# One of two subtractions per slice of the down-projection moves from VectorE to GpSimd

## The reference, cut to what matters

```
def conv_ffn(h, w_up, conv_w, conv_b, w_down):
    u = h @ w_up                       # 1024 x 5632
    c = conv_b + sum over j of conv_w[j] * u shifted by j
    a, g = jnp.split(c, 2, axis=-1)
    return (jax.nn.silu(a) * g) @ w_down      # z (1024 x 2816) @ w_down (2816 x 1024)

x = x + conv_ffn(rmsnorm(x, ffn_norm[l]), w_up[l], conv_w[l], conv_b[l], w_down[l])
```

## Time and profile before

| | |
|---|---|
| time, median of 3 runs | 1670.67 us (1668.64 to 1672.5) |
| the profiled execution: its time, its span | 1670.67 us, 1668.9 us |
| PE busy | 1614.7 us, 97% of the span |
| DVE busy | 1072.7 us, 64% |
| POOL busy | 946.5 us, 57% |
| ACT busy | 708.2 us, 42% |
| down stage: first to last PE matmul of L3146 | about 1454.6 to 1665.7 us |

### The profile page before, as it was taken

The page is one execution under the profiler, slowest core; times in us unless marked ns, Lnnn a source line. Parts: engine busy times, 40 slices in busy tenths (PEclk is TensorE's granted clock), DMA queues, the critical chain, the costliest instruction groups (busy, mean ns, idle before and its releaser), DMA issues.

```text
span 1668.9 us, 22838 instructions
## 1 busy us (share of the span) xinstructions
PE 1614.7 (97%) x8386; PEld 1329.5 (80%) x8386; DVE 1072.7 (64%) x1555; ACT 708.2 (42%) x1268; POOL 946.5 (57%) x705
## 2 busy tenths in 40 slices
PE   6999999998989999999999999999999999999999
PEld 5887878877778787888888887778888888888887
DVE  7555242357876493222655246888888888889897
ACT  5455465544554333333411233434433334454432
POOL 5642656544222287766344556999999999410041
PEclk9999999999999999999999999999999999999999
DMA  6113011002110233332455711222322222497244
GB/s 224 39 60 105 1 39 42 28 12 59 39 37 9 56 109 101 102 107 99 139 159 160 260 64 42 72 89 83 95 76 76 76 89 82 159 343 248 83 141 162
DMA packets 145146, 165.51 MB, mean 99 GB/s; under 512 B 16708, under 2 KB 97292, under 8 KB 145036
## 3 DMA queue, kind: packets, MB, share of 16 engines
q1 hardware_dynamic: 144604, 164.04, 30.5%
q10 hardware_dynamic: 432, 0.01, 0.0%
HBM read 131.40 MB, written 32.62 MB: 98 GB/s over the span
## 4 chain that ended last, share of the span: by engine, by line
PE 57%; POOL 5%; DVE 2%; issue 1%; ACT 0%; POOLq 0%; ACTq 0%
PE ps L3048 23%; PE ps L3146 11%; PE ps L2146 11%; PE ps L2186 7%; PE ps L2202 5%; POOL f_lo L2788 1%; POOL f_lo L1873 1%; PE ps L2137 1%; PE ps L2195 0%; POOL ffn_area L1888 0%; POOL ffn_area L1886 0%; POOL ffn_area L1883 0%; DVE attn_lo L2932 0%; POOL ffn_area L1885 0%; POOL ffn_area L2804 0%
## 5 line engine op out<-in xcount | busy, mean ns | idle before, releaser
L2788 POOL TENSOR_TENSOR f_lo<-ffn_area,f_hi 128x1024 fp32r<-128x1024 f32 x85 | 201.9, 2394 | 20.2 <-ACT f_hi L2663 20.2
L3048 PE MATMUL ps<-t_all,f_hi 128*128 128x512 f32 x528 | 164.3, 392 | 2.8 <-DVE t_all L2815 1.6
L2663 ACT ACTIVATE f_hi<-ffn_area 128x1024 fp32r<-128x1024 f32 x85 | 80.2, 946 | 184.5 <-PE ps L3048 169.8
L3146 PE MATMUL ps<-attn_lo 128*128 128x512 f32 x624 | 143.8, 390 | 0.0
L1873 POOL TENSOR_TENSOR f_lo<-ffn_area,f_hi 128x1024 fp32r<-128x1024 f32 (+1 forms) x42 | 97.5, 2325 | 69.4 <-ACT f_hi L1720 69.4
L3146 PEld LDWEIGHTS ps<-attn_lo 128*128 128x128 f32 x624 | 117.2, 188 | 24.5 <-issue 0.2
L3048 PE MATMUL ps<-act_hi,f_hi 128*128 128x512 f32 x336 | 133.3, 397 | 2.6 <-POOL f_lo L2788 2.6
L690 POOL TENSOR_SCALAR head_rstd<-head_ss 128x8 f32<-128x8 f32 (+2 forms) x42 | 10.4, 247 | 217.0 <-DVE head_ss L981 217.0
L3048 PE MATMUL ps<-act_hi,f_lo 128*128 128x512 f32 x336 | 132.3, 394 | 0.0
L3048 PE MATMUL ps<-act_lo,f_hi 128*128 128x512 f32 x336 | 131.3, 391 | 0.0
L1279 PE MATMUL ps<-w_hi,act_hi 128*128 128x512 f32 (+1 forms) x320 | 122.5, 383 | 5.8 <-DVE w_lo L506 2.6
(11 more groups left out here) (356 smaller groups left out, 4450.8 us busy)
## 6 DMA issues: line engine op xcount, KB each, us to landing
ffn_area<-in_w_up_dram SPq DMA_DIRECT2D x44, 512.0 KB, 5.2
gate<-gates SPq DMA_DIRECT2D x24, 512.0 KB, 3.7
ffn_area<-in_w_gate_dram SPq DMA_DIRECT2D x23, 512.0 KB, 5.1
z<-attn_out SPq DMA_DIRECT2D x22, 512.0 KB, 2.6
gates<-ffn_area SPq DMA_DIRECT2D x40, 256.0 KB, 2.1
t_raw<-in_w_down_dram SPq DMA_DIRECT2D x34, 256.0 KB, 6.3
attn_out<-in_x_dram SPq DMA_DIRECT2D x16, 512.0 KB, 6.2
f_raw<-in_w_down_dram SPq DMA_DIRECT2D x26, 256.0 KB, 4.9
```

Of the source, the lines that this page charges most:

```text
L2663: act.activation(part_place(p, part, f_hi, first_hi), part_source(p, part), ACT.Copy).then_inc(w_hi_done, 1)
L2788: pool.tensor_tensor(part_place(p, part, f_lo, first_lo), part_source(p, part), part_place(p, part, f_hi, first_hi).bitcast(F32), ALU.subt ...
L3048: ins = pe.matmul(out, w, a, start=(start and k == 0 and i == 0), stop=(stop and k == 3 and i == 2))
L3146: ins = pe.matmul(down_bank(i, t), z[a][:, t * P:(t + 1) * P], w[b], start=(k == 0 and n == 0), stop=(k == DEPTH - 1 and n == 2))
```

## The change

`z_low` moves from VectorE's stream to GpSimd's, for all 77 slices. VectorE keeps `w_low`. GpSimd's 20 additions, which stood in one row, now stand between the `z_low` of certain slices: `c11_x1` behind m = 17 to 20, `u3_made` behind m = 50 to 53, `c22_u3` and `c21_x1` in turn behind m = 61 to 68, `c12_x1` behind m = 69 to 72. No instruction is added or taken out, and the streams of TensorE, ScalarE and SyncE are the same instruction by instruction.

```diff
     def gpsimd(pool):
+        def z_low(m):
+            q, k = SLICES[m]
+            pool.wait_ge(z_hi_done, m + 1)
+            pool.tensor_tensor(operand(m, 1), block(DOWN[q], Z_OF[DOWN[q]], k), operand(m, 0).bitcast(F32), ALU.subtract
+                               ).then_inc(z_lo_done, 1)
...
-        for t in range(4):
-            c11_x1(t)
-        for t in range(4):
-            u3_made(t)
-        for t in range(4):
-            c22_u3(t)
-            c21_x1(t)
-        for t in range(4):
-            c12_x1(t)
+        for m in range(len(SLICES)):
+            z_low(m)
+            t = m - at_slice(P2, 0) - RING
+            if 0 <= t < 4:
+                c11_x1(t)
+            t = m - at_slice(P5, 0) - RING
+            if 0 <= t < 4:
+                u3_made(t)
+            n = m - at_slice(P4, 0) - RING
+            if 0 <= n < 8:
+                (c21_x1 if n % 2 else c22_u3)(n // 2)
+            elif 8 <= n < 12:
+                c12_x1(n - 8)
...
     def vector(dve):
-        def z_low(m):
...
-        def both_low(m):
-            z_low(m)
+        for m in range(4):
             w_low(m)
-
-        for m in range(4):
-            both_low(m)
         c12_sum(FT - 1)
         other_taps(FT - 1, 1)
-        both_low(4)
+        w_low(4)
         other_taps(FT - 1, 0)
-        both_low(5)
-        both_low(6)
+        w_low(5)
+        w_low(6)
         product(FT - 1)
         for m in range(7, len(SLICES)):
             combinations(m + AHEAD)
-            both_low(m)
+            w_low(m)
```

## The result

| | before | after |
|---|---|---|
| median of 8 runs | 1669.98 us (1667.15 to 1674.25) | 1679.32 us (1675.04 to 1681.79) |
| profiled execution: its time, its span | 1670.67, 1668.9 us | 1675.62, 1673.8 us |
| down stage, first to last matmul | 211.11 us | 220.70 us |

The ratio of after to before is 1.0052, with a 95% interval of 1.0036 to 1.0067. On 1669.98 us that is +8.7 us (+6.0 to +11.2); the medians themselves lie 9.3 us apart. The forecast was +7.8 us, 1678.5 us, slower with a chance of 0.76.

The account below looks back on a forecast made before the run. TensorE, busy 97% of the span, bounds the kernel; waits of 2.0 + 6.7 = 8.7 us replace 0.9, +7.8 us, so the span goes from 1668.9 to 1676.7, plus 1.8 around it 1678.5 us. Range 1671.5 to 1687.0.

Parts of the forecast that it names:

- The price, 0.60 + 1.11 = 1.71 us a pair: Down stage: VectorE and GpSimd instructions on SBUF take turns, 0.60 us for VectorE's and 1.11 for GpSimd's.
- The rival with a longer turn: Down stage: GpSimd's turn is longer than 1.11 us, so the time is 1684 to 1689 us; chance 0.11.
- Slices 0 to 21: Start of the down stage: TensorE does not wait, and 5 us of lead remain at slice 21.
- lead of `w_low`: Down stage: time from the end of a slice's `w_low` to TensorE's first matmul of it; 11.6 us at slice 60 before.
- Slices 22 to 30, lead 2 and no wait: Two combinations an iteration: 9 x 0.19 us lost, 1.2 for four `c11_y`, lead 2 us left.
- A loss before slice 50: Down stage: TensorE waiting before slice 50 was named as a sign that the forecast is wrong; no size given.
- Slices 31 to 50: Down stage: m = 31 to 41 gain 4.5 us, lead 6.5; m = 42 to 49 lose 1.3 and 0.8, lead 4.4.
- Slices 50 to 55, 2.0 us: At m = 50 to 53, iterations of 4.63 us with `u3_made` use up the lead; TensorE waits 2.0 us.
- Slices 61 to 73, 6.7 us: At m = 61 to 72, a second GpSimd turn loses 0.70 us an iteration; TensorE waits 6.7 us.
- the eight additions of `u4_c22_y` hide mostly under GpSimd's turns: At m = 61 to 72, of these VectorE PSUM additions (4.8 us) only a quarter, 1.2 us, is exposed.
- TensorE waits on `w_low`, not on `z_low`: Near slices 51 to 55 and 62 to 72: waits fall on VectorE's `w_low`, 0.7 us each in the latter.
- Waits saved: Slice 65 of the kernel before: its 0.9 us wait is replaced by the forecast waits of 8.7 us.

Follow-up runs that it names:

- experiment 3: The changed kernel with the four `c11_x1` additions behind m = 23 to 26 in place of 17 to 20; 1676.14 us, ratio 1.0052.
- experiments 4 and 6: GpSimd's 20 additions on VectorE: 4, against the kernel before, `z_low` on VectorE, 1666.53 us; 6, against the changed kernel, `z_low` on GpSimd, 1667.19 us.
- experiment 5: The changed kernel with `w_low` as a multiplication of one SBUF input by 0 in place of the subtraction; 1669.52 us, ratio 0.9999.

## Why the prediction was right, and the step that failed

**The price, 0.60 + 1.11 = 1.71 us a pair: right.** It was taken from four additions beside VectorE. `z_low`, which writes fp32r, steps at the same 1.70 to 1.71 in every stretch shown above. So the 1.30 us of the earlier trace rows was no hint of a longer turn: alone GpSimd steps by 1.25 us, and while both engines compete its part is 1.11. The rival with a longer turn is out.

**Slices 0 to 21: right.** The lead of `w_low` at m = 21 was predicted as 5 and is 4.7 us.

**Slices 22 to 30, lead 2 and no wait: the failed step.** It let GpSimd's 8 instructions up to `z_low(21)` pass, and then took one turn of GpSimd in each iteration, 2.92 us. GpSimd's timeline of the change:

```profile
1490.83 1.30 POOL L2827 TENSOR_TENSOR attn_out<-ffn_area,attn_out 128x512 f32<-128x512 f32 x1 [5.59 <-DMA attn_out<-x_kept]
...
1501.87 1.74 POOL L2821 TENSOR_TENSOR attn_lo<-f_raw,attn_lo 128x512 fp32r<-128x512 f32 x1
1503.57 3.48 POOL L2821 TENSOR_TENSOR t_all<-act_raw,t_all 128x512 fp32r<-128x512 f32 x2
1507.02 5.14 POOL L2821 TENSOR_TENSOR attn_lo<-act_raw,attn_lo 128x512 fp32r<-128x512 f32 x3
```

VectorE's:

```profile
1500.67 1.78 DVE L2936 TENSOR_TENSOR attn_lo<-f_raw,attn_lo 128x512 fp32r<-128x512 f32 x1
...
1505.80 1.80 DVE L2936 TENSOR_TENSOR t_all<-act_raw,t_all 128x512 fp32r<-128x512 f32 x1
...
1510.93 1.77 DVE L2936 TENSOR_TENSOR t_all<-act_raw,t_all 128x512 fp32r<-128x512 f32 x1
```

After `z_low(21)` at 1501.87 come five more without a pause, up to slice 26: GpSimd, held up by 5.59 us for x, still had its four additions to make among the next four `z_low`, and meanwhile ScalarE had written the high parts of the next slices (22 from 1496.44 us on). Until it had caught up, every VectorE instruction had a turn of GpSimd beside it, and an iteration took 3 x 1.71 = 5.13 us (1500.67, 1505.80, 1510.93), a loss of 2.4 each in place of 0.19. The lead of `w_low` fell from 4.7 at m = 21 to 2.3 at 22 and 0.1 at 23, while that of `z_low` grew from 3.5 to 9.3 at m = 26. The engine that isn't late takes turns from the one that is. In the chain above these are the VectorE pieces from 1500.67 on. TensorE lost 1.6 us; experiment 3, which moves the stop, gets it back. A combination that waited 2.0 us for a load stands just ahead (the DMA of the chain, 1485.28 to 1492.10); its part was not tried by itself. A loss before slice 50 was one of the forecast's own signs of being wrong, and here it is one.

**Slices 31 to 50: right.** Lead 5.5 at m = 42 (forecast 6.5 after 41), 4.2 at 49 (4.4).

**Slices 50 to 55, 2.0 us: the mechanism right, the size 3.2.** The iteration with `u3_made` was reckoned as 4.63 us. VectorE's `w_low` shows it:

```profile
1583.62 1.78 DVE L2936 TENSOR_TENSOR attn_lo<-t_raw,attn_lo 128x512 fp32r<-128x512 f32 x1
1585.32 0.68 DVE L2981 TENSOR_TENSOR ffn_area<-ps,ffn_area 128x512 f32<-128x512 f32 x1
...
1588.23 1.78 DVE L2936 TENSOR_TENSOR attn_lo<-t_raw,attn_lo 128x512 fp32r<-128x512 f32 x1
```

4.61 us, and the PSUM addition at 0.68 is indeed exposed. The missing 1.2 us are the steps from slices 53 and 54, 0.69 and 0.62: again `z_low` that had gathered behind an addition (three of them start at 1596.91, 1598.61 and about 1600.3), a second turn in iterations where one was counted.

**Slices 61 to 73, 6.7 us: 6.1.** Lead 3.4 at m = 60 (forecast 2.9), then 0.68 lost in each slice from 65 on, in place of 0.70. That the eight additions of `u4_c22_y` hide mostly under GpSimd's turns held: 3.4 + 6.1 = 9.5 us were used, and 12 x 0.70 + 1.2 = 9.6 were reckoned.

**TensorE waits on `w_low`, not on `z_low`: right** for the matmuls (10 waits). Four weight loads are put down to `z_low`, but each stands 0.03 us ahead of a matmul that waited too, three of them for `w_low`, and the lead of `z_low` was 5.6 us at slice 51 and 2.4 from 66 on: it had long been done.

**Waits saved.** The wait at slice 65 of before, 0.9 us by its row, is 1.2 by the starts. So the stage grew by 10.8 - 1.2 = 9.6 us, 1.8 more than the 7.8 forecast: +1.6 and +1.2 of gathered `z_low`, -0.6 at the end, -0.3 of the wait saved. The measured +8.7 (6.0 to 11.2) holds both. That the median after, 1679.32 us, lies only 0.8 from the forecast is luck in part: the stage lost 1.8 us more than forecast, and the 8 runs of before have a median 0.7 under the 1670.67 that the forecast started from.

## What to carry to other kernels

Where two engines take turns at SBUF, an instruction moved from VectorE costs VectorE the turn of the slower engine: 0.60 us went and 1.11 came. Idle time of the slower engine is no reason to give it more; with fewer instructions on it TensorE lost nothing (experiments 4 and 6). Reckon its turns by what has gathered in front of it, not by one per iteration, since it works off a backlog at the expense of an engine that may be the late one. Measure lost time by the distance of starts; the wait records gave half of it.

## What was unexpected of the hardware

- The one instruction with a single SBUF input that was tried, the `tensor_scalar` of experiment 5, loses the same 1.10 us to GpSimd as those with two: 0.42 becomes 1.52, 0.68 becomes 1.78.
- GpSimd's 128x512 addition of two SBUF inputs steps by 1.25 us alone (1.29 recorded), and adds only 1.11 to VectorE's stream while both are queued: a pair takes 1.71 us, 0.14 less than the 0.60 and 1.25 of the two alone. With a VectorE instruction of 0.33 us (experiment 5) the pair takes 1.44, which is 1.11 again.
- A wait for x or a `u2_y` on GpSimd costs later, not at once: what gathers behind it is worked off at 1.71 us per instruction of each engine, where GpSimd alone would have stepped by 1.25.
